# First attention of a two-layer decoder: rotated queries and keys transposed by VectorE blocks and an exchange through HBM on ScalarE's queue, in place of TensorE transposes

## The chip, the cores and the metric

The kernel runs on one core of one Trainium2 chip. The metric is the device time of one execution in microseconds (us). Before the change it is 923.49 us, the median of 3 runs (923.03 to 923.75).

## What is computed

The reference is a decoder trunk of two layers over 256 positions of width 1024. Each layer is half a SwiGLU block (inner width 2816), an attention, and another half SwiGLU block. The change touches only the attention of the first layer, a causal differential attention with 8 heads, each with two sub-queries and two sub-keys of 64 numbers. The first 16 numbers of each sub-query and sub-key are rotated by position:

```
qkv = u @ w_qkv
q, k, v = split(qkv)
q = apply_partial_rope(q.reshape(B, S, 8, 2, 64), cos, sin)
k = apply_partial_rope(k.reshape(B, S, 8, 2, 64), cos, sin)
s = einsum('bqhcd,bkhcd->bhcqk', q_blk, k) * scale
p = softmax(where(causal, s, -inf))
a = p[:, :, 0] - lam * p[:, :, 1]
o = einsum('bhqk,bkhe->bqhe', a, v)
```

## The kernel before

**Tiles and products.** The 256 positions are two blocks of 128 (`pos` 0 and 1). A weight matrix is streamed as units of 1 MB (128 rows by 2048 columns on chip), four of which are held at a time. Each unit is loaded by SyncE's DMA queue into `raw`, ScalarE makes a rounded upper part `w_hi` (L1367), and VectorE the remainder `w_lo` (L1750). TensorE then forms three products per tile (upper by upper, upper by lower, lower by upper): 12 matmuls of 128x512 for a unit and a block, made by `columns_pass` (L521). A unit's slot in `raw` is free when its `w_lo` is made, and its slot in `w_hi` and `w_lo` when TensorE has used it for both blocks.

**The projections.** The twelve units `U_QKV` to `U_QKV`+11 are walked in three parts (queries, keys, values), each with block 0 over its four units and then block 1. I call unit `U_QKV`+n "unit n". ScalarE copies each finished bank of 512 columns to `q_a`, `k_a` or `v_a` with a scale (`projection`, L1506), GpSimd rotates the queries and keys in place (`rope`, L1289 to L1298), half by half, and signals `s_rope`.

**The transposes.** Scores need queries and keys with the 64 numbers of a head down the partitions. `qk_transposes` waits for `s_rope` and turns 128x128 squares by multiplying with the identity (L582), eight for a block of queries or keys; ScalarE copies the results out of PSUM (`qk_transposed`, L1506 too) into `qT` and `kT_a`. The four calls stand between passes: queries of block 0 after the fourth pass of the keys part, queries of block 1 one pass later, keys of block 0 after the first pass of the values part, keys of block 1 after its third. `qk_ready(0)` ahead of the first scores, and `qk_ready(1)` before the first scores of block 1, wait for the copies.

**Attention.** `scores` (L745 puts in the mask, L752 the products) fills PSUM banks, VectorE takes maxima (L1954), ScalarE exponentials (`exps`, L1526), VectorE mixes the two probabilities (`combine`), TensorE transposes the mix (L582), ScalarE copies it (L1506) and TensorE multiplies by the values (`values`, L783). This is threaded between the passes of the values part, and later between those of the output projection.

**What sets the order.** Every engine runs one list, written out by hand; a wait holds all that follows on its engine. In the piece concerned, SyncE's list has only loads of weights, four units ahead. ScalarE's list is the sequence of `projection`, `split`, `qk_transposed` and `exps` after the line `u_v = U_QKV + 8`; VectorE's is eight splits in a row, then the first maxima.

**An exchange that is already there.** The inner activations of the SwiGLU blocks, and x ahead of most projections, are transposed without TensorE: VectorE turns 32x32 blocks of a 128x512 tile (`nc.vector.transpose`, L1803 and L1854), SyncE writes the tile to HBM in rows of 2 KB (`x_bounce`, L1043) and reads it back as four DMAs of 32 partitions with pieces of 512 bytes (`xn<-x_bounce`, L1055).

Of the kernel before, what the change touches and what calls it, by code (L numbers as in the profile page):

```python
# [30 lines left out]
F32 = mybir.dt.float32  # L31
# [7 lines left out]
P = 128  # L39
D = 1024  # L40
# [3 lines left out]
NPOS = SEQ // P  # L44
# [81 lines left out]
def trunk(nc, a, out):  # L126
    with ExitStack() as ctx:
# [3 lines left out]
        def sem(name):  # L131
            return ctx.enter_context(nc.semaphore(name))
# [82 lines left out]
        x_landed = [[xn[:, pos, BANK * j:BANK * (j + 1)] for j in range(2)] for pos in range(NPOS)]  # L215
        last_turned = [h[:, pos, CH:2 * CH] for pos in range(NPOS)]
# [4 lines left out]
        kT_a = [f[:, 4 * D:5 * D].rearrange("p (k s) -> p k s", k=HEADS // 2) for f in (att_1, att_2)]  # L221
# [49 lines left out]
        s_land_hi = [sem(f"s_land_hi{i}") for i in range(NPOS)]  # L271
        s_y = sem("s_y")
# [29 lines left out]
        def acc(pos, j):  # L302
            return 2 * pos + j
# [106 lines left out]
        def rotated(what, pos, j):  # L410
            return ROTATED[what] + half_no(pos, j)

        def qk_bank(which, pos, j):

            return acc(1, j) if (which, pos) == (1, 1) else 4 + 2 * (pos if which == 0 else 0) + j
# [57 lines left out]
        def _(pe):  # L473
# [442 lines left out]
            def qk_transposes(which, pos):  # L916

                for j in range(2):
                    pe.wait_ge(s_rope, rotated(("q_a", "k_a")[which], pos, j))
                    transposes(tiles((q_a, k_a)[which][:, pos, :], j), qk_bank(which, pos, j),  # L920
                               ("qkT", which, pos, j))

            def qk_ready(pos):
                for which in range(2):
                    for j in range(2):
                        in_sbuf(pe, ("qkT", which, pos, j))


            for part in range(3):
                u0 = U_QKV + 4 * part  # L930
                for pos in range(NPOS):
                    for i in range(4):
# [13 lines left out]
                        if (pos, i) == (0, 0):  # L946
                            qk_transposes(1, 0)
# [5 lines left out]
                        if (pos, i) == (0, 2):  # L953
                            qk_transposes(1, 1)
# [395 lines left out]
        def _(act):  # L1350
# [239 lines left out]
            def qk_transposed(which, pos):  # L1590
                for j in range(2):
                    dst = qT[:, 4 * j:4 * j + 4, own(pos)] if which == 0 else kT_a[j][:, :, own(pos)]
                    transposed(dst, qk_bank(which, pos, j), ("qkT", which, pos, j))
# [23 lines left out]
            qk_transposed(1, 0)  # L1617
            projection(2, 0, 0, v_a[:, 0, 0:BANK])
            exps(0, 0, 0)
            qk_transposed(1, 1)  # L1620
# [115 lines left out]
        def _(dve):  # L1736
# [229 lines left out]

            def combine(pos, r):
# [141 lines left out]
            for i in range(4, 12):  # L2109
                split(U_QKV + i)  # L2110
            maxima(0, 0, 0)
# [152 lines left out]
```

## Time and profile before

| | |
|---|---|
| median of the runs | 923.49 us (923.03 to 923.75) |
| the profiled execution | 923.58 us |
| its span, first to last instruction | 921.3 us |
| TensorE busy | 912.1 us, 99% of the span |
| VectorE, ScalarE, GpSimd busy | 569.0, 471.3, 90.0 us |
| granted TensorE clock, mean | 0.999 of full speed (2.4 GHz) |
| DMA | 200.75 MB, mean 218 GB/s |

The profiled execution lasted 923.58 us, of which 921.3 us are the span that the rows speak of and 2.3 us lie around it; it is 0.09 us above the median. The stretch of the change lies at 200 to 260 us of the span. Busy TensorE time is modelled and matmuls overlap, so a matmul's own 0.39 us isn't its cost; the distance between starts, or the chain's rows, give that.

### The profile page before, as it was taken

To read this page: it belongs to the slowest core of one execution; us is meant where nothing else is said; L and a number is where in the kernel's file an instruction comes from. 1 tells how busy PE (TensorE), PEld (TensorE's weight loads), DVE (VectorE), ACT (ScalarE), POOL (GpSimd) and SP (SyncE) were. 2 spreads that over 40 slices of the span, in tenths; PEclk is the share of its full clock that TensorE was granted. 3 is DMA by queue.
4 is the path that set the end of the run, shared out by engine and by line. 5 is a ranking of instruction groups with operands and counts; after the bars stand their busy time and mean duration, and the time that the engine had idled before them with its cause. 6 is when DMAs were issued, how large, how long until landed. Compare 5 with 4: busy or idle time off the path is not lost.

```text
span 921.3 us, 11586 instructions
## 1 busy us (share of the span) xinstructions
PE 912.1 (99%) x4235; PEld 748.6 (81%) x4235; DVE 569.0 (62%) x620; ACT 471.3 (51%) x638; POOL 90.0 (10%) x172
## 2 busy tenths in 40 slices
PE   8999999999999999999999999999999999999997
PEld 7888888888878888888888888888876788888885
DVE  5656663674587756664468566654578775756542
ACT  6544543475686645444445545434468655444431
POOL 1100006523311100000002000000030000000000
PEclk9999999999999999999999999999999999999999
DMA  9797777656532788876557878874673288887621
GB/s 313 244 299 237 242 252 232 214 190 235 184 93 90 229 270 253 255 260 221 186 175 242 236 248 251 300 251 164 203 271 96 92 273 259 269 253 284 224 81 46
DMA packets 166877, 200.75 MB, mean 218 GB/s; under 512 B 14840, under 2 KB 136768, under 8 KB 166832
## 3 DMA queue, kind: packets, MB, share of 16 engines
q1 hardware_dynamic: 165872, 199.27, 66.8%
q0 software_dynamic: 512, 0.36, 0.4%
q8 instruction: 27, 0.44, 0.2%
q10 hardware_dynamic: 448, 0.53, 0.2%
q14 instruction: 18, 0.15, 0.1%
HBM read 183.34 MB, written 16.78 MB: 217 GB/s over the span
## 4 chain that ended last, share of the span: by engine, by line
PE 97%; issue 1%; DMA 1%; ACT 0%; SPq 0%; DVE 0%; POOL 0%; POOLq 0%; ACTq 0%
PE bank L521 60%; PE bank L560 20%; PE bank L566 10%; PE bank L582 2%; PE bank L752 1%; PE bank L625 1%; PE bank L805 1%; PE bank L727 1%; PE bank L783 1%; DMA raw<-in_ffn_w_up 1%; PE bank L745 1%; DVE x L1817 0%; SPq L1072 0%; ACT junk L1386 0%; SPq L1162 0%
## 5 line engine op out<-in xcount | busy, mean ns | idle before, releaser
L1750 DVE TENSOR_TENSOR w_lo<-raw,w_hi 128x2048 fp32r<-128x2048 f32 x149 | 340.4, 2293 | 195.7 <-ACT w_hi L1367 195.5
L1367 ACT ACTIVATE w_hi<-raw 128x2048 fp32r<-128x2048 f32 x154 | 294.5, 1917 | 195.7 <-PE bank L566 100.0
L521 PE MATMUL bank<-w_hi,xT_hi 128*128 128x512 f32 x816 | 319.1, 391 | 0.0
L521 PE MATMUL bank<-w_lo,xT_hi 128*128 128x512 f32 x816 | 317.6, 389 | 0.0
L521 PE MATMUL bank<-w_hi,xT_lo 128*128 128x512 f32 x816 | 307.9, 389 | 0.0
L521 PEld LDWEIGHTS bank<-w_hi,xT_hi 128*128 128x128 f32 x816 | 153.2, 188 | 32.8 <-issue 0.7
L521 PEld LDWEIGHTS bank<-w_hi,xT_lo 128*128 128x128 f32 x816 | 153.1, 188 | 32.0
L521 PEld LDWEIGHTS bank<-w_lo,xT_hi 128*128 128x128 f32 x816 | 153.2, 188 | 31.4
L560 PE MATMUL bank<-w_hi,hT_hi 128*128 128x512 f32 x348 | 135.6, 390 | 0.0
L560 PE MATMUL bank<-w_lo,hT_hi 128*128 128x512 f32 x348 | 135.4, 389 | 0.0
L566 PE MATMUL bank<-w_hi,hT_lo 128*128 128x512 f32 x348 | 107.2, 389 | 0.0
L1422 ACT ACTIVATE hT_hi<-xn 128x512 f32 (+1 forms) x40 | 25.0, 625 | 112.3 <-DMA xn<-h_bounce 112.3
L566 PEld LDWEIGHTS bank<-w_hi,hT_lo 128*128 128x128 f32 x348 | 65.3, 188 | 13.6
L560 PEld LDWEIGHTS bank<-w_hi,hT_hi 128*128 128x128 f32 x348 | 65.3, 188 | 13.5
L560 PEld LDWEIGHTS bank<-w_lo,hT_hi 128*128 128x128 f32 x348 | 65.3, 188 | 13.5
L1201 POOL TENSOR_SCALAR ms<-ss 128x1 f32<-128x1 f32 x13 | 8.6, 665 | 595.9 <-ACT junk L1386 595.8
L1862 DVE TENSOR_TENSOR hT_lo<-xn,hT_hi 128x512 f32 (+1 forms) x40 | 27.6, 689 | 56.6 <-ACT hT_hi L1422 56.5
L1846 DVE SCALAR_TENSOR_TENSOR h<-bank,rstd,silu 128x256 f32<-128x256 f32 x88 | 41.5, 477 | 23.6 <-ACT silu L1416 23.5
L1416 ACT ACTIVATE silu<-bank,rstd 128x256 f32<-128x256 f32 x88 | 40.3, 462 | 27.3 <-PE bank L521 27.1
L1386 ACT ACTIVATE junk<-x 128x1024 bf16<-128x1024 f32 x13 | 13.7, 1055 | 44.4 <-DVE x L1797 23.1
L1854 DVE STREAM_TRANSPOSE silu<-h 128x512 f32<-128x512 f32 x40 | 28.5, 711 | 1.3
L560 PE MATMUL bank<-w_hi,xT_hi 128*128 128x512 f32 x64 | 26.3, 411 | 0.1
(182 smaller groups left out, 605.7 us busy)
## 6 DMA issues: line engine op xcount, KB each, us to landing
raw<-in_ffn_w_down SPq DMA_DIRECT2D x88, 512.0 KB, 5.4
raw<-in_ffn_w_gate SPq DMA_DIRECT2D x86, 512.0 KB, 6.0
raw<-in_ffn_w_up SPq DMA_DIRECT2D x86, 512.0 KB, 7.4
raw<-in_a_w_qkv SPq DMA_DIRECT2D x24, 512.0 KB, 5.8
h_bounce<-silu SPq DMA_DIRECT2D x40, 256.0 KB, 6.7
xn<-h_bounce SPq DMA_DIRECT2D x160, 64.0 KB, 3.1
xn<-x_bounce SPq DMA_DIRECT2D x64, 64.0 KB, 2.0
raw<-in_a_w_o SPq DMA_DIRECT2D x8, 512.0 KB, 5.3
```

The source lines that it names most:

```text
L521: mm = nc.tensor.matmul(bank[b][:, :], xs[:, kt, own(pos)], ws[:, slot(u), cols], start=(kt == 0 and i == 0), stop=(kt == KT - 1 and i == 2))
L560: nc.tensor.matmul(bank[acc(pos, j)][:, :], lhs_hi[:, kt, own(pos)], ws[:, slot(u), cols], start=(kt == 0 and i == 0), stop=False)
L566: mm = nc.tensor.matmul(bank[acc(pos, j)][:, :], lhs_lo[:, kt, own(pos)], w_hi[:, slot(u), cols], start=False, stop=(kt == n_kt - 1))
L582: mm = nc.tensor.transpose(bank[b][:, P * i:P * (i + 1)], src, ident[:, :])
L1367: nc.scalar.activation(w_parts(u)[0], raw[:, slot(u), :], ACT.Copy).then_inc(s_hi, 1)
L1386: nc.scalar.activation(junk[:, :], x[:, pos, :], ACT.Square, accum_out=ss[:, pos:pos + 1]).then_inc(s_ss, 1)
L1416: nc.scalar.activation(silu_of(pos, j, g), bank[acc(pos, j)][:, 0:CH], ACT.Silu, scale=rstd[:, pos:pos + 1]).then_inc(s_silu, 1)
L1422: nc.scalar.activation(hT_hi[:, bass.ds((g + turn) * 4, 4), own(pos)].rearrange("p t (q s) -> p t q s", q=4), landed[pos].rearrange("p (q ...
L1750: nc.vector.tensor_tensor(lo, raw[:, slot(u), :], hi.bitcast(F32), ALU.subtract).then_inc(s_lo, 1)
L1846: nc.vector.scalar_tensor_tensor(out=h[:, pos, CH * j:CH * (j + 1)], in0=bank[b][:, CH:2 * CH], scalar=rstd[:, pos:pos + 1], in1=silu_of(p ...
L1854: nc.vector.transpose(turned[pos].rearrange("p (q t s) -> p t q s", q=4, t=4), h[:, pos, :].rearrange("p (t q s) -> p t q s", t=4, q=4)).t ...
L1862: nc.vector.tensor_tensor(hT_lo[:, tile, own(pos)].rearrange("p t (q s) -> p t q s", q=4), landed[pos].rearrange("p (q t s) -> p t q s", q ...
```

## The change

The 32 identity products of the first attention's queries and keys, and the eight copies of their results, are gone. In their place:

- VectorE turns each half (128x512) of the rotated queries or keys in 32x32 blocks into `xn` (`qk_turn`).
- ScalarE's own DMA queue writes the halves to HBM (`qk_out`). For queries a half is four DMAs of 32 partitions, each with 512 pieces of 128 bytes; for keys it is one DMA with 128 pieces of 2 KB.
- ScalarE's queue reads them back (`qk_in`), four DMAs of 128 pieces of 512 bytes for each half, and TensorE waits for `s_qk_landed`. Queries land in the same layout as before. Keys keep blocks of 32 positions of different heads interleaved, so that the moving operand of a score product is read as runs of 32 numbers, 128 numbers apart.
- The keys' turn waits for the write of the same block's queries, which lie in the same buffer.

```diff
-        kT_a = [f[:, 4 * D:5 * D].rearrange("p (k s) -> p k s", k=HEADS // 2) for f in (att_1, att_2)]
+        k_wide = [f[:, 4 * D:5 * D] for f in (att_1, att_2)]
...
-                        kT = kT_a[head // 4][rows, head % 4, 0:keys] if layer == 0 else kT_b[rows, head // 4, 0:keys]
+                        if layer == 0:
+                            kT = k_wide[head // 4][rows, :].rearrange("p (a t s) -> p t a s", t=4, s=P // 4)
+                            kT = kT[:, head % 4, 0:keys * 4 // P, :]
...
             def qk_ready(pos):
-                for which in range(2):
-                    for j in range(2):
-                        in_sbuf(pe, ("qkT", which, pos, j))
+                pe.wait_ge(s_qk_landed[pos], 2 * 2 * H_READS * 16)
...
-                        if (part, pos, i) == (1, 0, 3):
-                            qk_transposes(0, 0)
-                        if (part, pos, i) == (1, 1, 0):
-                            qk_transposes(0, 1)
...
+            def qk_out(which, pos):
+
                 for j in range(2):
+                    act.wait_ge(s_qk_turned, half_no(pos, j) + 2 * NPOS * which)
+                    if which == 1:
+                        act.dma_start(k_bounce[pos, j], qk_turned[pos][j]).then_inc(s_k_bounced[j], 16)
+                        continue
+                    src = qk_turned[pos][j].rearrange("p (n i) -> p n i", n=16)
+                    for a4 in range(4):
+                        act.dma_start(q_bounce[pos, j, :, :, a4, :].rearrange("n s i -> s n i"),
+                                      src[32 * a4:32 * (a4 + 1), :, :]).then_inc(s_q_bounced[j], 16)
+
+            def qk_in(which, pos):
+
+                for j in range(2):
+                    if which == 0:
+                        act.wait_ge(s_q_bounced[j], 4 * 16 * (pos + 1))
+                    else:
+                        act.wait_ge(s_k_bounced[j], 16 * (pos + 1))
+                    for q in range(H_READS):
+                        rows = slice(32 * q, 32 * (q + 1))
+                        if which == 0:
+                            dst = qT[rows, 4 * j:4 * j + 4, own(pos)]
+                            src = q_bounce[pos, j, 4 * q:4 * q + 4, :, :, :].rearrange("t s a i -> s t (a i)")
+                        else:
+                            dst = k_wide[j][rows, BANK * pos:BANK * (pos + 1)].rearrange("p (a n) -> p a n", a=4)
+                            src = k_bounce[pos, j].rearrange("(a i) (q n) -> q i a n", a=4, q=H_READS)[q]
+                        act.dma_start(dst, src).then_inc(s_qk_landed[pos], 16)
...
             split(U_QKV + 4)
+            qk_out(0, 0)
             split(U_QKV + 5)
             projection(0, 1, 0, q_a[:, 1, 0:BANK])
             split(U_QKV + 6)
             split(U_QKV + 7)
+            qk_in(0, 0)
             projection(0, 1, 1, q_a[:, 1, BANK:D])
             projection(1, 0, 0, k_a[:, 0, 0:BANK])
+            qk_out(0, 1)
             projection(1, 0, 1, k_a[:, 0, BANK:D])
-            qk_transposed(0, 0)
             split(u_v)
-            qk_transposed(0, 1)
+            qk_in(0, 1)
+            qk_out(1, 0)
             split(u_v + 1)
             projection(1, 1, 0, k_a[:, 1, 0:BANK])
             split(u_v + 2)
+            qk_in(1, 0)
             split(u_v + 3)
...
+            def qk_turn(which, pos, j):
+
+                dve.wait_ge(s_rope, rotated(("q_a", "k_a")[which], pos, j))
+                if which == 1:
+                    dve.wait_ge(s_q_bounced[j], 4 * 16 * (pos + 1))
+                src = (q_a, k_a)[which][:, pos, BANK * j:BANK * (j + 1)]
+                nc.vector.transpose(qk_turned[pos][j].rearrange("p (q t s) -> p t q s", q=4, t=4),
+                                    src.rearrange("p (t q s) -> p t q s", t=4, q=4)).then_inc(s_qk_turned, 1)
```

**ScalarE's list from the split of unit 4 on.** `att` is the storage of queries, keys and values, `q_bounce` and `k_bounce` the buffers in HBM. Line numbers differ between the kernels: L1367 is L1357 after the change, L1506 is L1496. Before:

```order
L1367 ACTIVATE w_hi<-raw 128x2048 x2
L1506 ACTIVATE att<-bank,rstd 128x512
L1367 ACTIVATE w_hi<-raw 128x2048 x2
L1506 ACTIVATE att<-bank,rstd 128x512 x3
L1506 ACTIVATE att<-bank 128x4x128 x2
L1367 ACTIVATE w_hi<-raw 128x2048
```

After:

```order
L1357 ACTIVATE w_hi<-raw 128x2048
L1589 DMA q_bounce<-xn 32x16x32 x8
L1357 ACTIVATE w_hi<-raw 128x2048
L1496 ACTIVATE att<-bank,rstd 128x512
L1357 ACTIVATE w_hi<-raw 128x2048 x2
L1607 DMA att<-q_bounce 32x4x128 x8
L1496 ACTIVATE att<-bank,rstd 128x512 x2
L1589 DMA q_bounce<-xn 32x16x32 x8
L1496 ACTIVATE att<-bank,rstd 128x512
L1357 ACTIVATE w_hi<-raw 128x2048
L1607 DMA att<-q_bounce 32x4x128 x8
L1585 DMA k_bounce<-xn 128x512 x2
```

Eight DMA issues now stand between the splits of units 4 and 5, eight more after that of unit 7, eight before and ten after that of unit 8.

**VectorE's list from the lower parts of x to the first maxima.** Before:

```order
L1782 SCALAR_TENSOR_TENSOR xT_lo<-xn,gains,xT_hi 128x128 x8
L1750 TENSOR_TENSOR w_lo<-raw,w_hi 128x2048 x8
L1954 TENSOR_REDUCE mx<-bank 128x4 x2
L1959 TENSOR_SCALAR negm<-mx 128x8
L1954 TENSOR_REDUCE mx<-bank 128x4 x2
```

After:

```order
L1800 SCALAR_TENSOR_TENSOR xT_lo<-xn,gains,xT_hi 128x128 x8
L1991 STREAM_TRANSPOSE xn<-att 128x4x4x32 x2
L1768 TENSOR_TENSOR w_lo<-raw,w_hi 128x2048 x4
L1991 STREAM_TRANSPOSE xn<-att 128x4x4x32 x4
L1768 TENSOR_TENSOR w_lo<-raw,w_hi 128x2048 x4
L1991 STREAM_TRANSPOSE xn<-att 128x4x4x32 x2
L1972 TENSOR_REDUCE mx<-bank 128x4 x2
```

Two turns stand ahead of the eight splits, four in their middle, and two between them and the first maxima.

## Rows read from the trace of the kernel before

**Rows 1.** The page: busy time of two engines, and the chain by engine

```profile
PE 912.1 (99%) x4235; PEld 748.6 (81%) x4235; DVE 569.0 (62%) x620; ACT 471.3 (51%) x638; POOL 90.0 (10%) x172
...
PE 97%; issue 1%; DMA 1%; ACT 0%; SPq 0%; DVE 0%; POOL 0%; POOLq 0%; ACTq 0%
```

**Rows 2.** The chain in order of time, 190 to 290 us: start, us, what

```profile
222.21 0.87 PE bank L582 x8
...
226.69 10.93 PE bank L521 x48
...
241.68 1.09 PE bank L752 x16
...
247.36 0.87 PE bank L582 x8
...
258.68 1.06 PE bank L752 x8
```

**Rows 3.** Timeline of ScalarE, projections; in brackets idle time and its releaser

```profile
203.28 1.92 ACT L1367 ACTIVATE w_hi<-raw 128x2048 fp32r<-128x2048 f32 x1 [2.05 <-DMA raw<-in_a_w_qkv]
205.99 1.92 ACT L1367 ACTIVATE w_hi<-raw 128x2048 fp32r<-128x2048 f32 x1 [0.79 <-DMA raw<-in_a_w_qkv]
...
209.69 1.92 ACT L1367 ACTIVATE w_hi<-raw 128x2048 fp32r<-128x2048 f32 x1 [1.20 <-DMA raw<-in_a_w_qkv]
...
229.56 1.92 ACT L1367 ACTIVATE w_hi<-raw 128x2048 fp32r<-128x2048 f32 x1 [0.75 <-PE bank L521]
```

**Rows 4.** Timeline of VectorE: the lower part of unit 5

```profile
207.94 2.29 DVE L1750 TENSOR_TENSOR w_lo<-raw,w_hi 128x2048 fp32r<-128x2048 f32 x1 [0.42 <-ACT w_hi L1367]
```

**Rows 5.** SyncE's queue: DMA issues at the start, and of the exchange of x

```profile
7.62 0.51 SPq L1009 DMA_DIRECT2D raw<-in_ffn_w_up  x1
8.18 1.85 SPq L1009 DMA_DIRECT2D raw<-in_ffn_w_gate  x1
...
193.28 0.34 SPq L1043 DMA_DIRECT2D x_bounce<-h  x1
193.99 3.67 SPq L1055 DMA_DIRECT2D xn<-x_bounce  x8
```

**Rows 6.** Engines by stretch: stretch, us, busy by engine, clock, DMA share, GB/s

```profile
0.00:4.00 4.00, 2.42 (x11) 2.06 (x12) 0.17 (x1) 1.28 (x1) 0.74 (x7) 1.00 0.48 155
4.00:8.00 4.00, 3.57 (x24) 3.12 (x23) 2.80 (x5) 1.78 (x3) 0.00 (x0) 1.00 0.97 325
```

**Rows 7.** DMA, 206 to 217 us: queue, packets, MB, share of 16 engines

```profile
q1 hardware_dynamic: 2170, 4.18, 103.5%
```

**Rows 8.** The same, 194 to 197.6 us

```profile
q1 hardware_dynamic: 912, 0.61, 53.4%
```

**Rows 9.** The same, 153 to 156 us: SyncE's queue and GpSimd's beside it

```profile
q1 hardware_dynamic: 159, 0.57, 51.1%
q0 software_dynamic: 132, 0.19, 47.4%
```

**Rows 10.** Timeline of GpSimd: two DMA issues, near 149 us

```profile
149.07 0.56 POOL L1231 DMA_DIRECT2D gsub<-in_a_subln  x1
149.59 0.56 POOL L1232 DMA_DIRECT2D sinks<-in_b_sinks  x1
```

**Rows 11.** DMA issues: engine, op, count, KB each, median us to landing

```profile
xn<-x_bounce SPq DMA_DIRECT2D x64, 64.0 KB, 2.0
...
gsub<-in_a_subln POOLq DMA_DIRECT2D x1, 64.0 KB, 6.2
...
sinks<-in_b_sinks POOLq DMA_DIRECT2D x1, 8.0 KB, 6.7
```

**Rows 12.** Groups of instructions: busy us, mean ns, idle before

```profile
L1506 ACT ACTIVATE att<-bank 128x512 f32<-128x512 f32 x30 | 16.7, 602 | 7.1 <-PE bank L582 7.0
...
L1803 DVE STREAM_TRANSPOSE silu<-x 128x512 f32<-128x512 f32 x8 | 5.7, 712 | 0.3
```

**Rows 13.** Timeline near 256 us: the first product with the values, and what it waited for

```profile
256.86 0.52 PEld L783 LDWEIGHTS bank<-att 128*128 128x128 f32 x4 [0.35 <-ACT att L1506]
```

More of the change, by code:

```diff
@@ L215, in trunk @@
         x_landed = [[xn[:, pos, BANK * j:BANK * (j + 1)] for j in range(2)] for pos in range(NPOS)]
+        qk_turned = [[xn[:, pos, BANK * j:BANK * (j + 1)] for j in range(2)] for pos in range(NPOS)]
+        q_bounce = nc.dram_tensor("q_bounce", (NPOS, 2, 16, 32, 4, 32), F32).ap()
+        k_bounce = nc.dram_tensor("k_bounce", (NPOS, 2, P, BANK), F32).ap()
         last_turned = [h[:, pos, CH:2 * CH] for pos in range(NPOS)]
@@ L271, in trunk @@
         s_land_hi = [sem(f"s_land_hi{i}") for i in range(NPOS)]
+        s_qk_turned = sem("s_qk_turned")
+        s_q_bounced = [sem(f"s_q_bounced{j}") for j in range(2)]
+        s_k_bounced = [sem(f"s_k_bounced{j}") for j in range(2)]
+        s_qk_landed = [sem(f"s_qk_landed{pos}") for pos in range(NPOS)]
         s_y = sem("s_y")
@@ L411, in rotated @@
             return ROTATED[what] + half_no(pos, j)
-        def qk_bank(which, pos, j):
-            return acc(1, j) if (which, pos) == (1, 1) else 4 + 2 * (pos if which == 0 else 0) + j
         def o_bank(layer, pos, j):
@@ L750, in scores @@
                         rows = slice(HD * c, HD * (c + 1))
-                        kT = kT_a[head // 4][rows, head % 4, 0:keys] if layer == 0 else kT_b[rows, head // 4, 0:keys]
+                        if layer == 0:
+                            kT = k_wide[head // 4][rows, :].rearrange("p (a t s) -> p t a s", t=4, s=P // 4)
+                            kT = kT[:, head % 4, 0:keys * 4 // P, :]
+                        else:
+                            kT = kT_b[rows, head // 4, 0:keys]
                         mm = nc.tensor.matmul(bank[b][:, keys * i:keys * (i + 1)], qT[rows, head, own(pos)], kT,
@@ L914, in _ @@
             ffn(0, U_FFN1_0, "ln_ffn1_0", "ln_mix_0")
-            def qk_transposes(which, pos):
-                for j in range(2):
-                    pe.wait_ge(s_rope, rotated(("q_a", "k_a")[which], pos, j))
-                    transposes(tiles((q_a, k_a)[which][:, pos, :], j), qk_bank(which, pos, j),
-                               ("qkT", which, pos, j))
             def qk_ready(pos):
-                for which in range(2):
-                    for j in range(2):
-                        in_sbuf(pe, ("qkT", which, pos, j))
+                pe.wait_ge(s_qk_landed[pos], 2 * 2 * H_READS * 16)
             for part in range(3):
@@ L939, in _ @@
                                          name="ln_mix_0" if part == 0 and i < 2 else None)
-                        if (part, pos, i) == (1, 0, 3):
-                            qk_transposes(0, 0)
-                        if (part, pos, i) == (1, 1, 0):
-                            qk_transposes(0, 1)
                         if part < 2:
                             continue
-                        if (pos, i) == (0, 0):
-                            qk_transposes(1, 0)
                         if (pos, i) == (0, 1):
@@ L952, in _ @@
                             scores(0, 0, 1)
-                        if (pos, i) == (0, 2):
-                            qk_transposes(1, 1)
                         if (pos, i) == (1, 0):
@@ L1588, in projection @@
                 ins.then_inc(s_read[acc(pos, j)], 1)
-            def qk_transposed(which, pos):
+            def qk_out(which, pos):
                 for j in range(2):
-                    dst = qT[:, 4 * j:4 * j + 4, own(pos)] if which == 0 else kT_a[j][:, :, own(pos)]
-                    transposed(dst, qk_bank(which, pos, j), ("qkT", which, pos, j))
+                    act.wait_ge(s_qk_turned, half_no(pos, j) + 2 * NPOS * which)
[17 more added lines that the diff above has]
+                            src = q_bounce[pos, j, 4 * q:4 * q + 4, :, :, :].rearrange("t s a i -> s t (a i)")
+                        else:
+                            dst = k_wide[j][rows, BANK * pos:BANK * (pos + 1)].rearrange("p (a n) -> p a n", a=4)
+                            src = k_bounce[pos, j].rearrange("(a i) (q n) -> q i a n", a=4, q=H_READS)[q]
+                        act.dma_start(dst, src).then_inc(s_qk_landed[pos], 16)
             u_v = U_QKV + 8
@@ L1613, in _ @@
             split(u_v + 2)
+            qk_in(1, 0)
             split(u_v + 3)
             projection(1, 1, 1, k_a[:, 1, BANK:D])
-            qk_transposed(1, 0)
             projection(2, 0, 0, v_a[:, 0, 0:BANK])
+            qk_out(1, 1)
             exps(0, 0, 0)
-            qk_transposed(1, 1)
+            qk_in(1, 1)
             projection(2, 0, 1, v_a[:, 0, BANK:D])
@@ L2108, in _ @@
             landed_lo("ln_mix_0", 1)
-            for i in range(4, 12):
+            qk_turn(0, 0, 0)
+            qk_turn(0, 0, 1)
+            for i in range(4, 8):
                 split(U_QKV + i)
+            for which, pos in ((0, 1), (1, 0)):
+                for j in range(2):
+                    qk_turn(which, pos, j)
+            for i in range(8, 12):
+                split(U_QKV + i)
+            qk_turn(1, 1, 0)
+            qk_turn(1, 1, 1)
             maxima(0, 0, 0)
```

## The prediction

> **What bounds the kernel.** I read the page first: TensorE is busy 99% of the span, and it holds 97% of the chain that ended last [rows 1]. So time that TensorE no longer works is gained, and time that it newly waits is lost, one for one; VectorE (62%) and ScalarE (51%) count only where TensorE waits for them. I then read the chain in order of time for what a transpose and a pass really cost [rows 2], the timelines of ScalarE and VectorE for how far weights are ahead of TensorE [rows 3, 4], and the DMA rows for what a second queue will meet [rows 5 to 11]. The reader is to see in these that ScalarE's list carries the weights' upper parts, so whatever holds that list comes to TensorE a few microseconds later.
>
> **What is removed.** Four sets of eight identity products, each 0.87 us of the chain [rows 2], of which the first and the last are shown. With the slightly longer first matmul behind a set that makes 0.88, so 4 x 0.88 = **3.5 us** off TensorE. A pass of 12 matmuls is 10.93 / 4 = 2.73 us [rows 2]. ScalarE loses eight copies of 0.60 us, 4.8 us in all [rows 12], for which TensorE did not wait.
>
> **What is added, with its cover.**
> - VectorE: eight turns of 0.71 us [rows 12], 5.7 us. It is 62% busy [rows 1] and in the queries part it waits for ScalarE, so I cost them at nothing. Each waits for GpSimd's rotation and holds what is behind it: splits, and in the last case the first maxima, on which the exponentials and then the next products wait. With the cover gone that would be part of the late waits below.
> - ScalarE: 52 DMA issues. SyncE needs 0.34 us for a write and 3.67 / 8 = 0.46 us for a read of the same form [rows 5], so 48 x 0.46 + 4 x 0.34 = 23.4 us of its list, for 4.8 removed. Whether such an issue can go on while an earlier activation still runs no row shows: with it each group costs up to 1.9 us less, without it nothing less. In front of unit 5 are eight, 3.7 us.
> - The deadline there: TensorE's first transposes come after the four passes of the keys part on block 0, at 222.2 us [rows 2], so these passes start at 211.3, 214.0, 216.8 and 219.5 and need units 4 to 7. From the start of unit 5's upper part to the end of its lower part are 207.94 + 2.29 - 205.99 = 4.24 us [rows 3, 4]. The upper part may therefore start at 214.0 - 4.2 = 209.8 us at the latest, for 205.99 now: 3.8 us of slack. Eight unhindered issues, begun when unit 4's activation starts at 203.28 [rows 3], end at 207.0. They fit, if nothing slows them.
> - DMA: for queries of one block 2 x 4 x 512 pieces of 128 bytes, 256 for each of 16 engines. Pieces of 2 KB take 1.035 x 16 x 11 us / 2170 = 84 ns of an engine [rows 7]; a mix around 670 bytes takes 0.534 x 16 x 3.6 / 912 = 34 ns [rows 8]. No row has 128 bytes to HBM. The line through both gives 12 ns, and the price of the mix, 34, is the other end; I take 20, nearer the line since time falls with size. That is 256 x 20 ns = 5.1 us of all engines for a block (3.1 to 8.7).
> - Keys read in runs of 32 by the 64 score products: nothing as far as rows tell, since none has such an operand. If it doubled them, it would be 2 x 1.09 us for block 0 and 4 x 1.06 us for block 1 [rows 2], of which one round each is shown, so 0 to 6.4 us; I take 0.
>
> **Where I choose.** When the first query writes are issued, at 203 to 207 us, the DMA engines are full: 103.5% at 206 to 217 us [rows 7], and units 5, 6 and 7 are still on their way (ScalarE waits for DMA in front of each [rows 3]). Two facts decide.
>
> First, a queue takes only so much ahead. At 8.18 us SyncE's issue of 512 KB took 1.85 us, and the one before it 0.51 [rows 5]. By then the code had issued some 4.0 MB, and 4 x 155 + 4 x 325 KB = 1.9 MB had moved [rows 6]. The rest, mostly in pieces of 1 KB, is about 120 pieces for an engine. I take 120 as what a queue holds; a block of queries is 256.
>
> Second, how quickly does a second queue empty beside a full one? At 153 to 156 us GpSimd's queue and SyncE's shared the engines, 47.4% and 51.1% [rows 9]. The small `sinks` landed at 149.59 + 6.7 = 156.3 us, the DMA before it on that queue at 149.07 + 6.2 = 155.3 [rows 10, 11]: 1.0 us for 8 pieces of 64 bytes on each engine, 125 ns a piece, when a small piece alone should take some 20. That reads like one small piece for each large piece of the other queue. Here the other's pieces take 84 ns, so a query piece would take 84 + 20 = 104 ns as long as weights are queued. The eighth issue ends when 256 - 120 = 136 pieces are gone: 136 x 104 ns = 14.1 us after 203.3, at 217.4 us. Unit 5 is then split at 217.4 and ready at 221.7, against 214.0: TensorE waits **7.7 us**.
>
> The Trainium skill ("DMA: Bandwidth & Descriptors", "Queues, rings and completion order") says that a DMA engine goes round the queues and changes only between packets of about 9 to 17 descriptors. If both queues have packets of like count, the sum stays; if a packet of weights is filled by bytes and has only two pieces, sixteen query pieces would go in 2 x 84 + 16 x 20 ns, 30 ns each, and my first rival would follow. The same page ("Specifications") gives 512 bytes as the least size for full rate, with a read-modify-write below it; no row here shows one. Were a query piece for that reason as dear as the mix, 118 ns in place of 104, the stall would be 9.6 us and the end 930.
>
> **Sum.** Against the execution's own 923.6 us: 923.6 - 3.5 + 7.7 = 927.8, which is also the sum against the median, 0.1 lower. Later exchanges find TensorE later by 4 to 5 us but their own chains are tight: behind unit 8's split ScalarE has 8 x 0.46 + 2 x 0.34 = 4.4 us of issues before unit 9, which it began at 229.56 [rows 3] and may begin no later than 231.5 on the shortened schedule; keys of block 0 then need a write, eight issues and 2.0 us to land [rows 11]. I give these 0 to 3 us and take little. **Forecast 928 us.**
>
> **Rivals.**
> 1. *The exchange is hidden.* Issues stay at 0.46 us, the queries' pieces go quickly between the weights, and unit 5 starts at 207. For it: the slack of 3.8 us, and x is already exchanged in this way with 2.0 us to landing [rows 11]. Against it: that exchange is on the same queue as the weights, in pieces of 512 bytes or more, and never 256 an engine. Time: 923.6 - 3.5 = 920.1, up to 921.6 where a small wait returns, such as the copy of probabilities on ScalarE for which `values` already waited 0.35 us [rows 13]; if ScalarE isn't earlier there, the gain is lost at that point.
> 2. *Equal shares of time.* Rows 9 can be read as half the time to each queue. Then the query writes take 10.2 us from 203.3, and unit 6, with 6.4 us of transfer left for its landing at 209.69 [rows 3], lands at 214.8, where 212.5 is the latest: 2.3 us of wait, 922.4 us. Between 921.7 and 925.3 lies also the case in which only the keys' landing is late, by 1 to 4 us.
> 3. *The keys' runs of 32 are slow.* 920.1 + up to 6.4 = 926.5; it shows as longer score products.
> 4. *The work doesn't leave TensorE.* The order of the new kernel has none of the four sets, so I exclude this.
>
> **Numbers.** The eight issues of the first group have 209.8 - 203.3 = 6.5 us before TensorE waits; 3.5 us more and the gain is spent, so the sign turns at 10.0 us for the eight, 1.25 us each. Chances: forecast 0.45 (925.3 to 932), rival 1 0.35, rival 2 and late keys alone 0.17, rival 3 0.03. A measurement of this kernel tells 0.2%, 1.85 us, from no change: under 921.6 is faster, over 925.3 slower. That gives faster 0.35, same 0.17, slower 0.48. The range runs from 920.2, rival 1 with almost nothing returned, to 932, the forecast with its 3 us of later waits and the dearer piece, which leaves out about 2 in 10. The likeliest case alone spans 925.3 to 932.
>
> **What would show it.** Right: on ScalarE's queue, the fifth to eighth `q_bounce` issues near 205 us last 2 to 4 us each; the split of unit 5 starts near 217; TensorE has an idle stretch of 6 to 9 us near 214 us, released by VectorE's `w_lo`; no L582 row reads `att`. Wrong: `q_bounce` issues all near 0.46 us, `w_lo` of unit 5 ready by 213 us. Then, if TensorE still stands still, its idle time ends on a DMA (late weights, rival 2; late `k_bounce`, at the first scores near 238 us). A round of scores that takes over 1.1 us of the chain would show rival 3.

## The result and the profile after

The changed kernel takes **937.17 us**, the median of 4 runs (935.94 to 940.74), beside 923.4 us before: a ratio of 1.0156, 95% interval 1.0144 to 1.0168. It is slower by 13.8 us, outside the forecast range. The profiled execution lasted 936.75 us, its span 934.9 us; 13.6 us of span are to be found. One execution of a later version fell out of line, with 1310 us at a mean granted clock of 0.655, and no ratio below counts it.

The page, busy time and the chain by engine, as [rows 1]:

```profile
PE 915.2 (98%) x4203; PEld 749.7 (80%) x4203; DVE 574.4 (61%) x628; ACT 466.4 (50%) x630; POOL 93.4 (10%) x172
...
PE 88%; DVE 4%; DMA 3%; issue 2%; ACT 1%; ACTq 1%; SPq 1%; POOL 0%; POOLq 0%
```

TensorE has 32 instructions fewer and is busy 3.1 us longer. It held 97% of the chain and holds 88%. The first says that its own work became slower, the second that it waits. The chain in order of time (start, us, what) shows both:

```profile
203.69 0.53 ACTq L1589
...
204.25 0.55 ACTq L1589
...
204.83 2.98 ACTq L1589
...
207.85 3.29 ACTq L1589
...
215.63 1.92 ACT w_hi L1357
...
217.57 2.30 DVE w_lo L1768
...
219.92 27.48 PE bank L524 x108
247.40 3.73 issue
251.13 1.01 PE bank L748 x2
252.14 2.01 PE bank L759 x16
254.15 0.97 PE bank L748 x2
255.12 1.72 PE bank L759 x16
...
270.18 1.06 PE bank L759 x8
```

Read downward: the query writes (L1589) hold ScalarE. The four shown are the second to the fifth; the first (0.34 us) lies beneath unit 4's activation at 203.31. Unit 5 is split at 215.63, where [rows 3] have 205.99. 108 matmuls follow (seven passes of the keys part and two of the values part), then TensorE stands still for 3.73 us, then block 0's scores take nearly twice the 1.09 us of [rows 2]. Block 1's take 1.06, as before. The same chain in the kernel before has for block 0, around the rows of [rows 2]:

```profile
241.23 0.45 PE bank L745 x2
...
242.77 0.54 PE bank L745 x2
243.31 1.09 PE bank L752 x16
```

ScalarE's timeline has the first group of writes in one row, and the first four of them in two when smaller windows are asked for:

```profile
203.31 12.22 ACTq L1589 DMA_DIRECT2D q_bounce<-xn  x8
...
203.31 0.91 ACTq L1589 DMA_DIRECT2D q_bounce<-xn  x2
...
204.25 3.56 ACTq L1589 DMA_DIRECT2D q_bounce<-xn  x2
...
215.63 1.91 ACT L1357 ACTIVATE w_hi<-raw 128x2048 fp32r<-128x2048 f32 x1 [10.41 <-issue]
...
226.16 7.64 ACTq L1589 DMA_DIRECT2D q_bounce<-xn  x8
...
237.77 0.93 ACTq L1585 DMA_DIRECT2D k_bounce<-xn  x2
...
239.99 1.31 ACTq L1607 DMA_DIRECT2D att<-k_bounce  x3
```

Next the engines by stretch. Behind each duration stand the busy times of TensorE, its weight loads, VectorE, ScalarE and GpSimd, then the granted clock:

```profile
214.00:220.00 6.00, 0.14 (x2) 0.08 (x1) 2.34 (x2) 4.37 (x4) 1.80 (x1) 0.90 0.53 120
220.00:225.00 5.00, 5.00 (x12) 3.94 (x13) 4.66 (x2) 2.30 (x2) 4.92 (x4) 0.50 0.91 287
...
247.40:251.00 3.60, 0.00 (x0) 0.00 (x0) 2.29 (x3) 0.69 (x1) 2.87 (x5) 0.80 1.02 362
251.00:256.80 5.80, 5.67 (x37) 3.69 (x37) 1.70 (x4) 1.09 (x7) 0.00 (x0) 0.53 0.83 328
```

And of the kernel before:

```profile
217.00:222.00 5.00, 5.00 (x23) 4.10 (x23) 0.00 (x0) 0.49 (x1) 2.46 (x7) 1.00 0.93 340
```

TensorE worked 0.14 us of the first stretch, and in the next its clock is 0.50, 1.2 GHz in place of 2.4: 12 matmuls in 5 us, where the kernel before has 23. The same follows the second idle time. Both sets of slow work lie just behind an idle stretch.

The second idle time has no releaser in the profile ("issue"). What TensorE's list has there are the waits for the mask and for the landed queries and keys. The queue of ScalarE still moves 4 packets between 250 and 251 us, a read of keys took up to 7.6 us to land, and the scores start at 251.13; in the two versions below whose profile names a releaser at this place, it is `att<-k_bounce`.

The sum up to the first product with the values (256.86 us in [rows 13], 268.43 now): the products removed -3.5; idle ahead of unit 5 +5.9; 108 matmuls at partly half clock, 27.48 for 24.59 us (108 x 10.93 / 48, [rows 2]), +2.9; idle ahead of the scores +3.7; two rounds of masks and scores, 5.71 us for 3.17, +2.5; small things +0.1. That is 11.6 us. The other 2.0 us come much later, at two places where the trace before has no wait: by the starts of its matmuls, TensorE loses 0.6 us near 512 us behind `hT_lo`, and 1.4 us near 694 us behind a rotation by GpSimd. At both, ScalarE waits longer for the landing of an exchange of x (`xn<-x_bounce`): 2.3 us for 0.8, and up to 3.4 for 0.9.

Last, who had the DMA engines while the eight query writes were being issued. Here are three answers of the DMA view (queue, packets, MB, share of 16 engines; q1 is SyncE's queue with the weights, q10 ScalarE's), of one microsecond each. From 204.3, a microsecond after the first issue:

```profile
q1 hardware_dynamic: 203, 0.39, 104.3%
```

From 208.3:

```profile
q1 hardware_dynamic: 187, 0.36, 93.5%
q10 hardware_dynamic: 183, 0.02, 14.9%
```

From 210.3, where the weights' queue has run short:

```profile
q10 hardware_dynamic: 1147, 0.14, 92.4%
q1 hardware_dynamic: 76, 0.12, 32.4%
```

From the first issue at 203.3 to 207.0 us no query piece moves at all. Then, as long as weights fill their queue, one small piece goes for each large one. Where they leave a gap, the small ones need 0.924 x 16 us / 1147 = 12.9 ns each. The kernel before has no such gap: its weights take 99.8% or more in each microsecond from 207.3 to 216.3 us. From 214 us on the gap is the stall's own doing. A slot for unit 9 is free when unit 5's `w_lo` is made, and SyncE issues its load at 219.89 us in place of 210.26.

### The profile page after: what moved, and what is told of

Same layout as the page of the kernel before. It is cut to its first block, busy times and chain, and to the rows that moved or that the text cites. A ratio compares the mean times of both kernels' runs of the same rounds, so it can differ in the third digit from the quotient of the medians.

```text
span 934.9 us, 11555 instructions
## 1 busy us (share of the span) xinstructions
PE 915.2 (98%) x4203; PEld 749.7 (80%) x4203; DVE 574.4 (61%) x628; ACT 466.4 (50%) x630; POOL 93.4 (10%) x172
## 4 chain that ended last, share of the span: by engine, by line
PE 88%; DVE 4%; DMA 3%; issue 2%; ACT 1%; ACTq 1%; SPq 1%; POOL 0%; POOLq 0%
PE bank L524 54%; PE bank L563 18%; PE bank L569 9%; PE bank L759 2%; PE bank L585 2%; ACTq L1589 1%; PE bank L628 1%; DVE w_lo L1768 1%; ACT w_hi L1357 1%; DMA x_bounce<-silu 1%; PE bank L812 1%; PE bank L748 1%; SPq L1045 1%; PE bank L790 1%; DMA raw<-in_ffn_w_up 1%
## 5 line engine op out<-in xcount | busy, mean ns | idle before, releaser
L1357 ACT ACTIVATE w_hi<-raw 128x2048 fp32r<-128x2048 f32 x154 | 294.1, 1916 | 198.6 <-PE bank L569 100.0
L524 PE MATMUL bank<-w_hi,xT_hi 128*128 128x512 f32 x816 | 320.2, 392 | 5.9 <-DVE w_lo L1768 5.9
L563 PEld LDWEIGHTS bank<-w_hi,hT_hi 128*128 128x128 f32 x348 | 65.3, 188 | 13.6
L1394 ACT ACTIVATE xT_hi<-xn,gains 128x128 fp32r<-128x128 f32 x64 | 20.2, 389 | 12.7 <-DMA xn<-x_bounce 12.7
```

Of the source, the lines that this page charges most:

```text
L524: mm = nc.tensor.matmul(bank[b][:, :], xs[:, kt, own(pos)], ws[:, slot(u), cols], start=(kt == 0 and i == 0), stop=(kt == KT - 1 and i == 2))
L563: nc.tensor.matmul(bank[acc(pos, j)][:, :], lhs_hi[:, kt, own(pos)], ws[:, slot(u), cols], start=(kt == 0 and i == 0), stop=False)
L1357: nc.scalar.activation(w_parts(u)[0], raw[:, slot(u), :], ACT.Copy).then_inc(s_hi, 1)
L1394: nc.scalar.activation(squares(x_parts(name)[0], pos, kt), landed_tile(pos, kt), ACT.Copy, scale=gain_column(name, kt)).then_inc(s_land_hi ...
```

## The experiments

The first theory: the small pieces of the writes are so many that they fill ScalarE's queue beside full-rate weights and block its list; late keys and a slower TensorE clock are separate costs on top. All ratios are against the kernel before, run on the same chip.

### The kernel before with extra writes

Four kernels add writes of x to a spare buffer, which nothing reads, to ScalarE's list.

```diff
             split(U_QKV + 4)
+            extra_writes(8)
             split(U_QKV + 5)
```

**Eight writes in pieces of 128 bytes**, like the first query group.

> The kernel before, with nothing changed but eight more DMAs on ScalarE's queue between the splits of units 4 and 5: they write x's first block to a buffer that nothing reads, in the form of the queries' writes (each 512 pieces of 128 bytes). Theory: these alone hold ScalarE for about 12 us, TensorE waits about 6 us for unit 5 and loses about 3 us more by the half clock: 923.5 + 9 = 932 to 933 us. Rival (the wait comes from what follows, the reads back and the waits for them): no wait at unit 5, below 925 us.

Measured 931.77 us, ratio 1.0087 (1.007 to 1.0104). Its ScalarE timeline, and TensorE's idle time before unit 5:

```profile
203.24 12.69 ACTq L1602 DMA_DIRECT2D extra_out<-x  x8
```

```profile
220.32 0.79 PE L524 MATMUL bank<-w_hi,xT_hi 128*128 128x512 f32 x1 [6.34 <-DVE w_lo L1761]
```

The stall stands alone here, with nothing else of the change: 6.3 us of wait and a slow matmul behind it (0.79 us), 8.3 us in all. So a stall of 6 us costs about 2 us more than itself. No further wait follows in its trace.

**The same bytes and the same eight DMAs in pieces of 512 bytes**, a quarter of the pieces (64 for each engine).

> The same eight extra DMAs at the same place with the same bytes, but each in 128 pieces of 512 bytes, 64 pieces for an engine in all. Theory (a queue holds about 120 pieces for an engine): all eight fit, the issues take 0.4 to 0.5 us each, 3.7 us together, unit 5 keeps its slack, 923.5 to 924.5 us. Rival (the bytes, or the number of DMAs in flight, fill the queue): the fifth to the eighth issue again last 1 us and more, and TensorE waits at unit 5: above 926 us.

Measured 923.68 us, ratio 1.0002 (0.9992 to 1.0012).

```profile
203.79 4.96 ACTq L1602 DMA_DIRECT2D extra_rows<-x  x8
```

4.96 us fit the 6.5 us that the prediction had found. So the stall of 12 us comes neither from the bytes nor from the count of DMAs, but from the pieces: how many they are, or how small, which this pair doesn't separate. The eight weren't unhindered, as was expected (3.7 us): the seventh alone took 1.59 us, until the first pieces had moved. What held it was not followed.

**Two writes in pieces of 128 bytes**, 64 pieces an engine.

> The kernel before with two extra writes in pieces of 128 bytes (64 pieces for each DMA engine) behind unit 4's split. Theory (a queue holds about 120 pieces an engine and blocks only beyond that): both issues take about 0.45 us, unit 5 is split as early as before, and the time stays within 0.2% of the kernel before. Rival (any write in small pieces blocks the issue while weights are streaming): the issues take 1.5 us each or more.

Measured 923.5 us, ratio 1.0002 (0.9992 to 1.0011); the two issues took 0.90 us together. So small pieces don't block an issue by their size; it takes more of them. In the changed kernel the first two take 0.91 us as well (203.31), the third 0.55 and the fourth 2.98: it ends at 207.81, 0.8 us after the first piece has moved. With eight extra writes it is the same, 0.59 us for the third and 2.80 for the fourth. So 96 pieces an engine go in at once. In the second query group (226.16) and in the next experiment four issues, 128 pieces, go in before any piece has moved, in 2.76 and 2.26 us, and the fifth is held, for 3.17 and 2.37 us. The 120 of the prediction lies between.

**Eight writes of 128 bytes at a quieter place**, near 241 us, where weights run dry 3 us later.

> The kernel before with the same eight extra writes in pieces of 128 bytes, 256 pieces for each DMA engine, placed about 241 us behind a projection's copy. Theory (the price of a small piece is one turn of the other queue plus its own 20 to 35 ns): with less weight traffic beside it the eight issues take 4 to 6 us in place of 12.7. Rival (a piece of 128 bytes to HBM costs some 100 ns by itself): again 11 to 13 us.

Measured 923.37 us, a single execution.

```profile
241.05 6.32 ACTq L1602 DMA_DIRECT2D extra_out<-x  x8
```

Half of 12.7 us, just above the 4 to 6 that were expected, and far from the rival's 11 to 13. Again nothing moves for 3 us while weights are queued. From 245 to 246 us, with the weights nearly gone:

```profile
q10 hardware_dynamic: 1123, 0.14, 90.3%
q1 hardware_dynamic: 7, 0.02, 4.1%
```

That is 12.9 ns a piece again: a 128-byte piece is cheap by itself, and the wait for the other queue is what makes it dear.

### One part of the change, or another form of it

**Keys alone exchanged.** Queries go through TensorE as before.

```diff
+                        if (part, pos, i) == (1, 0, 3):
+                            q_transposes_a(0)
...
-            qk_out(0, 0)
...
-            qk_in(0, 0)
...
-            qk_out(0, 1)
```

> Only the keys go through HBM; the queries stay with TensorE's identity products and ScalarE's copies. Theory (the small query pieces fill ScalarE's queue and hold its list): no wait at unit 5 and no half clock behind it, the sets of products that remain cost 2 x 0.88 us, so 923.5 - 1.8 = 921.7 us if the keys land in time, and up to 923.5 if block 0's keys still come late by 1 to 2 us. Rival (the exchange as such, whatever its pieces, is too slow for this place): the keys of block 0, whose round trip begins last, still hold the first scores by some 3.7 us, and with the slow clock behind that the time is 926 to 928 us.

Measured 927.8 us (923.15 to 928.78, 5 runs), ratio 1.005 (1.0034 to 1.0067). The profile is of the shortest execution; TensorE waits 1.8 us for keys in it, just what the removed products gave:

```profile
241.77 0.59 PE L748 MATMUL bank<-mask_a,identb 128*128 128x512 bf16 x2 [1.79 <-DMA att<-k_bounce]
```

Behind this idle time the mask products take 0.59 us and the scores 1.16, at full clock, as in the kernel before. Rounds of scores at full speed with strided keys also end the rival that these were slow. The other four executions, 927.04 to 928.78 us, lie where the experiment's own rival put them (926 to 928), or just above: even without the query writes, the exchange of the keys comes too late here. Their mean granted clock is 0.995 to 0.997, for 0.999 in the profiled one, which fits a longer wait with slow work behind it; none of them was profiled.

**Queries in rows of 2 KB.** They are written by two DMAs a block, 8 pieces an engine each, read back in the keys' form into the storage of q, and copied into columns by ScalarE.

```diff
-                    src = qk_turned[pos][j].rearrange("p (n i) -> p n i", n=16)
-                    for a4 in range(4):
-                        act.dma_start(q_bounce[pos, j, :, :, a4, :].rearrange("n s i -> s n i"),
-                                      src[32 * a4:32 * (a4 + 1), :, :]).then_inc(s_q_bounced[j], 16)
+                    act.dma_start(q_bounce[pos, j], qk_turned[pos][j]).then_inc(s_q_bounced[j], 16)
```

> As the changed kernel, but the queries are written in 128 rows of 2 KB by one DMA for each half (2 issues in place of 8 for a block), land as blocks of 32 positions in the storage of the rotated queries, and ScalarE puts them in columns by four copies of about 0.6 us; the output is the same. Theory: the issues of the first group take 0.7 us in all instead of 12.2, unit 5 is in time, both long waits and the half clock go, and what is left is the gain of 3.5 us less small waits: 920 to 922 us. Rival (it is the number of bytes added to a full DMA, or ScalarE's number of issues, not the pieces): 4 MB more on a busy DMA and 40 issues still delay weights or keys, and the time stays above 928 us.

Measured 933.15 us (4 runs), ratio 1.0104 (1.0087 to 1.0121): a miss by 11 us, and in the rival's range. The part on unit 5 came true, the rest didn't. ScalarE's timeline has no stall, and TensorE's shows where it went:

```profile
203.72 0.82 ACTq L1590 DMA_DIRECT2D q_bounce<-xn  x2
```

```profile
249.07 1.01 PE L750 MATMUL bank<-mask_a,identb 128*128 128x512 bf16 x2 [9.25 <-DMA att<-k_bounce]
```

Key reads are issued at 236.9 to 240.7 us, behind ScalarE's waits for queries, and beside the output projection's weights (SyncE issues these from 231.69 on); key DMAs took up to 8.5 us to land. Late keys are a second cause of its own, which the first stall had partly covered: here the scores would have come at 239.8 us and wait for keys until 249.07, in the changed kernel from 247.40 until 251.13.

**TensorE kept working through the idle stretches.** The changed kernel with extra identity products on an unused bank, 52 before unit 5's pass and 32 before the first scores.

```diff
+                            if (part, pos, i) == (1, 0, 1):
+                                for _ in range(52):
+                                    nc.tensor.transpose(bank[7][:, 0:P], ident[:, :], ident[:, :])
```

> The changed kernel with 52 extra identity products on an idle bank before unit 5's first pass and 32 before the first scores, so that TensorE works through the two idle stretches; the same work otherwise. Theory (the clock that falls behind an idle stretch is a cost of its own, 2.9 us on the keys part's passes and 2.4 us on block 0's scores): the granted clock stays near 1.0 at 214 to 226 us, both score rounds of block 0 take 1.6 us of each kind as in the kernel before, and the time is 931 to 933 us. Rival (slow score rounds are the strided keys, and the slower passes are waits): the time stays at 936 to 938 us with score rounds of 2 us at full clock.

Measured 932.57 us (931.79 to 933.75), ratio 1.0098 (1.0081 to 1.0115), as expected: **84 useless products make it 4.6 us faster.** The stall on ScalarE is the same, 12.23 us.

```profile
214.00:220.00 6.00, 5.82 (x54) 5.58 (x52) 2.31 (x2) 4.34 (x4) 1.77 (x1) 1.00 0.52 117
220.00:226.00 6.00, 6.00 (x27) 4.96 (x28) 5.25 (x3) 3.02 (x3) 5.78 (x6) 1.00 0.90 290
```

The clock stays at 1.00, 27 matmuls in 6 us, and the score rounds take 0.59 us (mask) and 1.16 us (products). The clock is shown as a cause. The 4.6 us are not its price, though: the first product with the values starts 2.9 us earlier than in the changed kernel (265.50 for 268.43), since new waits of 1.2 us (`w_lo` of a values unit) and 0.8 us (the copied probabilities) stand against the 5.4 us, and the late waits of 2 us are absent.

**The first writes behind unit 7's split.**

```diff
             split(U_QKV + 4)
-            qk_out(0, 0)
             split(U_QKV + 5)
...
             split(U_QKV + 7)
-            qk_in(0, 0)
+            qk_out(0, 0)
             projection(0, 1, 1, q_a[:, 1, BANK:D])
             projection(1, 0, 0, k_a[:, 0, 0:BANK])
+            qk_in(0, 0)
```

> The changed kernel with the first group of query writes issued behind the split of unit 7 in place of unit 4, and the reads later by one projection. Theory (a block of query pieces fills the queue wherever weights fill the DMA engines): the eight issues again take 8 to 12 us, now behind unit 7's split, and hold the projection copy and the next group; TensorE's wait moves there or to the keys, and the time is 930 to 938 us. Rival (only the place before unit 5 is bad, since it has 3.8 us of slack): the stall hides behind three split units and the time is 925 to 928 us.

Measured 937.34 us, ratio 1.0146 (1.0129 to 1.0163). Unit 5 no longer waits; TensorE idles 3.67 us at a values unit (236.98) and 8.52 us before the scores:

```profile
252.93 1.01 PE L748 MATMUL bank<-mask_a,identb 128*128 128x512 bf16 x2 [8.52 <-issue]
```

The eight issues take 8.6 us at their new place, as expected. Moving the stall only moves the wait.

**Keys alone, with the output projection's weights held back.**

```diff
+            sp.wait_ge(s_qk_landed[0], 2 * H_READS * 16)
             rows(U_WO_A, 4, a["a_w_o"][0])
```

> Keys alone exchanged (queries by TensorE as before), with SyncE waiting for block 0's keys before it loads the weights of the output projection. Theory (late keys are the key reads beside full-rate weights): the wait for the keys at the first scores goes to below 0.5 us, the time is 921 to 923 us and the runs agree within 0.3%. Rival (the keys' own chain, turn, write, read, is too long without any other traffic): the wait stays near 1.8 us and the time at 926 to 928 us.

Measured 927.15 us (926.4 to 928.65), ratio 1.0034 (1.0022 to 1.0047). Half a miss: no wait is left at the first scores, so the keys' lateness was that traffic; but the time is the rival's. The held weights now meet block 1's keys. ScalarE waits for their write and issues their reads ahead of a copy and exponentials, and TensorE waits behind those:

```profile
248.66 4.40 ACTq L1620 DMA_DIRECT2D att<-k_bounce  x8
253.11 0.69 ACT L1509 ACTIVATE att<-bank,rstd 128x512 f32<-128x512 f32 x1 [6.08 <-PE bank L585]
```

```profile
258.93 2.07 PE L790 MATMUL bank<-att 128*128 128x128 f32 x8 [3.69 <-ACT att L1509]
```

The eight products take 2.07 us, twice as long as at full speed: the clock is 0.60 in the 5.2 us from 256.8.

**Both, reordered.** Queries in rows of 2 KB, keys of block 0 read ahead of block 1's queries, copies of queries later on ScalarE, weights held as above.

> Queries in rows of 2 KB with two issues a block and copied into columns on chip, keys of block 0 read ahead of block 1's queries, copies of queries later, and the output projection's weights held until block 0's keys have landed. Theory (few large pieces keep the queue free, and the keys wait only for traffic): no wait at unit 5, under 1 us at the first scores, 920 to 922 us, which is faster than the kernel before. Rival (the chain of copies and issues on ScalarE is itself too long before the scores): 2 to 5 us of wait at the first scores, 924 to 928 us.

Measured 930.37 us, ratio 1.0068 (1.0047 to 1.0089). A miss for the same reason: no wait at unit 5 nor at the first scores, but one at the first product with the values, and slow work behind it:

```profile
259.90 2.08 PE L792 MATMUL bank<-att 128*128 128x128 f32 x8 [6.71 <-ACT att L1500]
```

### A version that gains

So far each version's trouble was one thing: ScalarE's list has both the deadlines and the waits for landings. SyncE issues nothing between 217.5 and 230.2 us in the kernel before. This version leaves the writes (2 KB rows, two issues a block) on ScalarE's queue and puts the reads on SyncE's, between the two matrices; each write has a semaphore of its own. The output projection's weights thereby come behind both blocks' keys, so two things change at once; the version before, which held them behind block 0's keys alone, shows that this by itself is not enough.

```diff
             columns(U_QKV, 6, a["a_w_qkv"][0], "ln_mix_0")
+            qk_in(0, 0)
+            qk_in(1, 0)
+            qk_in(0, 1)
+            qk_in(1, 1)
             rows(U_WO_A, 4, a["a_w_o"][0])
```

> Queries and keys exchanged in rows of 2 KB; the writes stay on ScalarE's queue (two issues a block), the reads move to SyncE's, between the last weights of the projections and those of the output projection, which are thereby loaded after both blocks' keys. Theory (what is left of the loss in the reordered kernels is that ScalarE's list waits for landings and issues reads while weights fill the DMA engines): no wait at unit 5, none over 0.5 us at the first scores or the first product with the values, the keys land in 2 to 3 us, and the time is 920 to 922 us. Rival (the weights of the output projection come too late when loaded from about 248 us on): waits of 1 to 4 us between 256 and 290 us and a time of 922 to 927 us.

Measured 922.24 us (10 runs), ratio 0.9988 (0.9978 to 0.9998). TensorE's waits from 200 us on, total, times, longest:

```profile
PE bank L792 <- ACT att L1522: 1.0, 1, 1.0
PE bank L587 <- POOL xn L1314: 0.7, 1, 0.7
PE bank L732 <- DVE hT_lo L1811: 0.7, 1, 0.7
```

Key DMAs land in 2.0 us in the median and 3.1 at most. The waits at unit 5 and at the first scores are gone, as expected; the 1.0 us at the first product with the values is above the 0.5 that was. It was of my making, two copies of queries in front of the copied probabilities, so one more:

```diff
             exps(0, 0, 0)
+            q_columns(1)
             projection(2, 0, 1, v_a[:, 0, BANK:D])
             exps(0, 0, 1)
-            q_columns(1)
```

> The kernel with the reads on SyncE's queue, and the two copies of block 1's queries moved on ScalarE from behind the second group of exponentials to behind the first, where ScalarE idles 2.9 us. Theory (the 1.0 us that TensorE waits for the copied probabilities ahead of the first product with the values comes from these copies): that wait goes, and the time falls from 922.2 to 921.3 us, 920.8 to 921.8. Rival (the copies are not what was late, or the time comes back as later waits for landings near 499 and 681 us): the time stays at 922 to 922.5 us.

Measured **921.15 us** (920.66 to 922.1, 10 runs), ratio **0.9975** (0.9965 to 0.9984), as expected, and faster than both kernels. It is a gain of 0.25%.

```profile
PE 909.0 (99%) x4203; PEld 745.5 (81%) x4203; DVE 574.2 (62%) x628; ACT 469.2 (51%) x634; POOL 90.6 (10%) x172
...
PE 95%; issue 1%; DMA 1%; DVE 1%; SPq 1%; ACT 1%; POOL 0%; POOLq 0%; ACTq 0%
```

TensorE's busy time is now 3.1 us below [rows 1]. The first product with the values starts earlier than in [rows 13] (256.86):

```profile
253.50 1.16 PE L792 MATMUL bank<-att 128*128 128x128 f32 x8
```

So the removed products are worth 3.4 us there, as costed. Of this 2.1 us are left at the end; 0.9 us go in one late wait near 680 us for a rotation of GpSimd, and some of the rest was not followed.

## Why the prediction was wrong

**Right.** Direction and first mechanism of the forecast: the fourth and fifth query writes last 2.98 and 3.29 us (I had named the fifth to the eighth, which last 3.29, 1.13, 2.57 and 0.60), unit 5's split starts at 215.6 (forecast 217.4), and TensorE idles until `w_lo` comes. The removed products were costed at 3.5 us and are worth 3.4 in the last version. No wait of TensorE ends on a turn of VectorE. Strided keys cost nothing. That eight writes in pieces of 128 bytes block ScalarE where the same bytes in pieces of 512 don't was shown by itself.

**The first term, the stall, was too large by 1.8 us** (5.9 for 7.7), and that it came so close was partly luck. "I take 120 as what a queue holds" was about right: 96 go in at once, and at two places 128. "One small piece for each large piece" holds, 183 and 187 in a microsecond, but only while the weights' queue is full; ahead of it lie 3.7 us in which nothing of the new queue moves, and behind it gaps in which a piece takes 12.9 ns. The prediction had neither, and the two errors went in opposite directions. With the line through [rows 7, 8] I had 12 ns for a piece and took 20; the line was right.

The Trainium skill ("DMA: Bandwidth & Descriptors", "Queues, rings and completion order") has an engine change queues behind packets of about 9 to 17 descriptors. I had drawn two cases from it, packets of like count and packets of weights filled by bytes, with 16 small pieces for two large ones. The trace has one for one over a microsecond: that rules out the second case and fits the first, so it doesn't contradict the page. The same page's least size for full rate ("Specifications", 512 bytes) agrees in direction: 12.9 ns for 128 bytes is 9.9 bytes a nanosecond, where the weights of [rows 7] have 23 (4.18 MB in 2170 pieces of 84 ns).

**The step that failed is the sentence "I give these 0 to 3 us and take little".** It held three things.
- Keys late at the first scores, 3.7 us. I priced their landing at 2.0 us from [rows 11], a median over exchanges on the weights' own queue. My own one-for-one rule, used for the query writes, was not used for the key reads a page later: 64 pieces an engine beside full weights, up to 7.6 us to land. I also let the second query group go unhindered, and it took 7.64 us.
- TensorE's clock, 5.4 us (2.9 and 2.5). I priced an idle stretch at its own length. After 5.9 us and after 3.7 us of idling the work behind it ran at 1.2 GHz for several microseconds, so each stall cost 2.5 to 2.9 us on top of its length. With the stretches filled, the clock stayed at 1.00. The profile before, all at 0.999, has no such stretch, so the range should have been open upward.
- 2.0 us of late waits behind other exchanges' landings. They are absent in the kernel before, in the one with filled stretches and in the one with eight extra writes, and are there in several others, the fastest among them. Their cause stays open.

Together with the too large first term and 0.1 us of small things: -1.8 + 3.7 + 5.4 + 2.0 + 0.1 = 9.4 us. With the 4.2 us of the forecast (7.7 - 3.5) that makes the 13.6 us by which the span grew.

**The rivals.** The first, that it is hidden, was wrong for this form but describes the last version, whose pieces are few. Equal shares of time did not come about: beside full weights the query writes had 14.9% and the weights 93.5%. "Late keys alone" had 1 to 4 us, and with equal shares 0.17 of the chance, as an alternative to the stall; it was an addition to it. I had set up as exclusive what could add up.

## What to carry to other kernels

Count a new DMA in pieces for each engine, not in bytes: a group that exceeds what a queue takes at once (here 96 to 128 pieces an engine) holds its issuing engine while another queue's weights stream, and everything with a deadline in that list is late. Put waits for landings and reads on an engine whose list has no deadlines in that stretch, and see which bulk transfer will be running when they are issued. Price a stall of TensorE of 4 to 6 us at its length and 2 to 3 us more, since here the work behind it ran at half clock.

## What the runs showed of the hardware that was not expected

- A second queue's first piece moved 3.1 to 3.7 us after its first issue while another queue streamed, in pieces of 128 bytes at either place (207.0 us for 203.3, 244.1 for 241.05) and in pieces of 512 bytes (207.5 for 203.8).
- A queue took 96 pieces of 128 bytes for each DMA engine in 1.5 us and held the issue of the next 32 for 2.98 us; at two other places it took 128 in 2.3 and 2.8 us before any had moved, and held the next.
- 128-byte writes to HBM took 12.9 ns of a DMA engine where the other queue had a gap (16 engines at 92% and 90%).
- The granted clock fell to 0.5 (1.2 GHz) with idle stretches of TensorE of 3.7 and 5.9 us, and not with one of 1.8 us; with useless products in the long stretches it stayed at 1.0.
